# Moving eighteen conditioning broadcasts, four LayerNorm affines and one last affine in a two-layer encoder kernel

## The reference

```python
c_act = jax.nn.silu(c)
for layer in range(DEPTH):
    mod = c_act @ cond_w[layer] + cond_b[layer]
    sh_m, sc_m, g_m, sh_f, sc_f, g_f = [m[:, None, :] for m in jnp.split(mod, 6, axis=-1)]
    h = x * (1.0 + sc_m) + sh_m
    y = mixer(h)
    x = layer_norm(ALPHA * x + g_m * y, ln_w[layer, 0], ln_b[layer, 0])
    h = x * (1.0 + sc_f) + sh_f
    y = feed_forward(h)
    x = layer_norm(ALPHA * x + g_f * y, ln_w[layer, 1], ln_b[layer, 1])
```

## Time and profile before

| | us |
|---|---|
| Runs | 1716.56, 1714.35, 1717.05; median 1716.56 |
| The profiled execution | 1716.56 |
| Its span | 1714.7 |
| PE busy in the span | 1615.6 (94%) |
| DVE busy | 1286.5 (75%) |
| ACT busy | 1008.3 (59%) |
| POOL busy | 134.3 (8%) |

### The profile page before, as it was taken

How to read it: one execution, slowest core, us unless ns; L and a number is a source line. 1 busy time by engine, 2 the same in 40 slices (tenths; PEclk the granted TensorE clock), 3 DMA queues, 4 the chain that set the end, 5 groups by cost and what they waited for, 6 DMA issues and landing times.

```text
span 1714.7 us, 20084 instructions
## 1 busy us (share of the span) xinstructions
PE 1615.6 (94%) x7810; PEld 1292.7 (75%) x7810; DVE 1286.5 (75%) x1162; ACT 1008.3 (59%) x867; POOL 134.3 (8%) x92
## 2 busy tenths in 40 slices
PE   4888999999999999789999999999999999999996
PEld 1774766788868777578888888888888888888875
DVE  1384638655467665788898898898898888998987
ACT  0432225444444544357777777777777777777775
POOL 0330402020001001210000000000000000000004
PEclk8997999999999999889999999999999999999998
DMA  9347996965445444479999999999999999999994
GB/s 328 138 150 269 320 356 206 297 218 197 169 157 175 154 148 171 147 258 389 384 382 386 375 389 382 374 388 373 381 390 370 385 389 370 389 385 361 388 377 157
DMA packets 234370, 515.33 MB, mean 301 GB/s; under 512 B 8936, under 2 KB 40960, under 8 KB 234176
## 3 DMA queue, kind: packets, MB, share of 16 engines
q1 hardware_dynamic: 228272, 491.99, 78.6%
q0 software_dynamic: 3008, 10.20, 1.9%
q10 hardware_dynamic: 2992, 11.79, 1.9%
HBM read 507.15 MB, written 13.11 MB: 303 GB/s over the span
## 4 chain that ended last, share of the span: by engine, by line
PE 87%; DVE 7%; issue 2%; ACT 2%; DMA 2%; POOL 0%; POOLq 0%; SPq 0%; DVEq 0%
PE bank L759 26%; PE bank L761 25%; PE bank L760 25%; PE bank L738 2%; PE bank L924 2%; DMA ring<-in_cond_w 2%; PE bank L1188 1%; PE bank L754 1%; DVE arena L1791 1%; DVE w_part L1650 0%; ACT w_part L1315 0%; PE bank L1170 0%; PE bank L855 0%; DVE w_lo L1661 0%; PE bank L1179 0%
## 5 line engine op out<-in xcount | busy, mean ns | idle before, releaser
L1661 DVE TENSOR_TENSOR w_lo<-ring,w_hi 128x2048 fp32r<-128x2048 f32 x336 | 765.0, 2290 | 104.4 <-ACT w_hi L1544 102.9
L1544 ACT ACTIVATE w_hi<-ring 128x2048 fp32r<-128x2048 f32 x334 | 640.5, 1918 | 196.8 <-PE bank L761 187.1
L759 PE MATMUL bank<-w_lo,heT_hi 128*128 128x512 f32 x896 | 353.9, 395 | 3.8 <-DVE w_lo L1661 2.2
L761 PE MATMUL bank<-w_hi,heT_hi 128*128 128x512 f32 x896 | 349.7, 390 | 0.0
L760 PE MATMUL bank<-w_hi,heT_lo 128*128 128x512 f32 x896 | 348.9, 389 | 0.0
L1650 DVE TENSOR_TENSOR w_part<-ring,w_part 128x1024 fp32r<-128x1024 f32 x148 | 185.5, 1262 | 180.1 <-ACT w_part L1315 173.1
L1315 ACT ACTIVATE w_part<-ring 128x1024 fp32r<-128x1024 f32 (+1 forms) x162 | 168.9, 1049 | 233.5 <-PE bank L761 228.2
L759 PEld LDWEIGHTS bank<-w_lo,heT_hi 128*128 128x128 f32 x896 | 168.3, 188 | 39.0 <-issue 5.9
L761 PEld LDWEIGHTS bank<-w_hi,heT_hi 128*128 128x128 f32 x896 | 168.2, 188 | 35.9
L759 PE MATMUL bank<-w_part,hT_hi 128*128 128x512 f32 (+1 forms) x448 | 178.2, 398 | 17.8 <-DVE w_part L1650 12.3
L760 PEld LDWEIGHTS bank<-w_hi,heT_lo 128*128 128x128 f32 x896 | 168.4, 188 | 33.5
(11 more groups left out here) (342 smaller groups left out, 1586.7 us busy)
## 6 DMA issues: line engine op xcount, KB each, us to landing
ring<-in_moe_w_up SPq DMA_DIRECT2D x224, 1024.0 KB, 8.5
ring<-in_moe_w_down SPq DMA_DIRECT2D x112, 1024.0 KB, 7.9
ring<-in_cond_w SPq DMA_DIRECT2D x24, 2048.0 KB, 9.1
ring<-in_ffn_w_up SPq DMA_DIRECT2D x22, 1024.0 KB, 7.9
ring<-in_od_w_in SPq DMA_DIRECT2D x8, 2048.0 KB, 8.0
ring<-in_ev_w_in SPq DMA_DIRECT2D x5, 2048.0 KB, 12.4
ring<-in_ffn_w_down SPq DMA_DIRECT2D x5, 2048.0 KB, 7.9
ring<-in_od_w_in SPq DMA_DIRECT2D x8, 1024.0 KB, 8.0
```

The source lines that it names most:

```text
L759: mm(bank, lhs[0], rhs[1], start=start, stop=False)
L761: return mm(bank, lhs[0], rhs[0], start=False, stop=stop)
L1544: f(w_hi[:, n % 3], half_landed(act, it, u, half), ACT.Copy) \
L1661: tt(w_lo[:, buf], at, w_hi[:, buf].bitcast(F32), ALU.subtract).then_inc(S["w_lo"], 1)
```

## The change

- `MIX_COND` and `END_COND` go. Their 18 pieces are spread elsewhere: (0, 6) and (0, 7) after level 3, (0, 8) and (0, 9) after level 4; ten pieces in feed-forward up, one after each unit from unit 1 to unit 10; two in feed-forward down, ahead of units 2 and 4; (1, 10) and (1, 11) after `od_qk` of heads 1 and 2. The ScalarE evictions stand at the matching places of its stream.
- The affines of stages 0 and 1 move from their places in the loops into `stage_end`: after the transposed copies DVE makes one more low part, the affine of tile 0, one more low part, the affine of tile 1, and waits for it. ScalarE's wait before the gates goes.
- In stage 3 the affine of tile 0 moves from DVE to POOL, with a semaphore `first_done`, on which SyncE waits before it sends out tile 0. DVE does tile 1.

The hunks of `pe_order()` are left out below; they list the same moves.

```diff
@@ -127,9 +127,10 @@
 BATCH_OF = {key: b for b, batch in enumerate(COND_BATCHES) for key in batch}
 
 ROWS_LEVEL = 1
-LEVEL_COND = {2: (4, 5)}
-MIX_COND = (6, 7, 8, 9)
-END_COND = (((0, 10), (0, 11), (1, 0), (1, 1), (1, 2), (1, 3)), tuple((1, u) for u in range(4, 10)), ((1, 10), (1, 11)))
+LEVEL_COND = {2: (4, 5), 3: (6, 7), 4: (8, 9)}
+UP_COND = {0: (0, 10), 1: (0, 11), 2: (1, 0), 3: (1, 1), 4: (1, 2), 5: (1, 3), 6: (1, 4), 7: (1, 5), 8: (1, 6), 9: (1, 7)}
+DOWN_COND = {0: (1, 8), 2: (1, 9)}
+OD_COND = {0: 10, 1: 11}
 
 
 def stream_units():
...
@@ -711,7 +714,7 @@
             over_loop(sp, over_count(sp), over_item)
             for t in range(NT):
 
-                sp.wait_ge(S["ln_done"], 3 * NT + t + 1)
+                sp.wait_ge(S["ln_done" if t else "first_done"], 3 * NT + 1 if t else 1)
                 sp.dma_start(out[0, t * P:(t + 1) * P, :], xs[:, t]).then_inc(S["out_done"], 16)
             sp.wait_ge(S["out_done"], 16 * NT)
 
@@ -1029,12 +1032,8 @@
                 last.then_inc(full, 1)
             cond_rows(len(cond_order) - rows_next[0])
             turn(1, lambda half, t: taken(pe, "pv", t) if half else pe.wait_ge(S["mix_ready"], t + 1), (2, 3, 0, 1))
-            for u in MIX_COND:
-                cond(0, u)
             project(("ev_out", 0), 1)
             project(("ev_out", 1), 1, steps=LAST)
-            for key in END_COND[0]:
-                cond(*key)
             turn(2, h_ready(1), BY_TILE[:2])
 
             def down(kind, lhs, n_units, n_chunks, between):
@@ -1075,6 +1074,8 @@
             for u in range(FFN // 256):
                 project(("ffn_up", u), 2, steps=None if u else FIRST,
                         second=None if u else lambda: turn(2, h_ready(1), BY_TILE[2:]))
+                if u - 1 in UP_COND:
+                    cond(*UP_COND[u - 1])
                 if u:
                     ffn_turn(u - 1)
 
@@ -1082,11 +1083,11 @@
 
                 if i == 1:
                     ffn_turn(FFN // 256 - 1)
+                if i > 1 and i - 2 in DOWN_COND:
+                    cond(*DOWN_COND[i - 2])
                 taken(pe, "ffn_T", min(2 * i + 1, FFN // 256 - 1))
 
             down("ffn_down", (ffT_hi, ffT_lo), 6, FFN // P, ffn_between)
-            for key in END_COND[1]:
-                cond(*key)
             turn(3, h_ready(2), BY_TILE[:2])
             def weighted_values(g):
 
@@ -1112,6 +1113,8 @@
             for h in range(RH):
                 project(("od_qk", h), 3, steps=None if h else FIRST,
                         second=None if h else lambda: turn(3, h_ready(2), BY_TILE[2:]))
+                if h - 1 in OD_COND:
+                    cond(1, OD_COND[h - 1])
                 if h:
                     weighted_values(h - 1)
                 project(("od_v", h), 3)
@@ -1144,8 +1147,6 @@
                     taken(pe, "ret_yT", i, t)
 
             down("od_out", (yT_hi, yT_lo), 4, RH * RV // P, od_between)
-            for key in END_COND[2]:
-                cond(*key)
             turn(4, h_ready(3), BY_TILE)
 
             pe.wait_ge(S["nw_lo"], 2)
@@ -1280,9 +1281,7 @@
 
                 if l == 1:
 
-                    if u < 4:
-                        act.wait_ge(S["h_ready"], 4)
-                    elif u < 10:
+                    if u < 10:
                         act.wait_ge(S["h_ready"], 8)
                     else:
                         act.wait_ge(S["ln_done"], 4)
@@ -1425,22 +1424,15 @@
                 for t in range(NT):
                     act.wait_ge(S["resid_var"], NT * stage + t + 1)
                     f(rstd[:, t:t + 1], aggr[:, t, 1:2], ACT.Sqrt, bias=eps_ln).then_inc(S["resid_rstd"], 1)
-                    keys = END_COND[stage] if stage < 3 and t == 0 else ()
-                    for key in keys[:1]:
-                        cond(*key)
                     act.wait_ge(S["norm_in"], NT * stage + t + 1)
                     f(xs[:, t], hs[:, t], ACT.Identity, bias=shift_n[:, t:t + 1], scale=rstd[:, t:t + 1]) \
                         .then_inc(S["normed"], 1)
-                    for key in keys[1:]:
-                        cond(*key)
                     if turn_rows:
                         turned(stage + 2, BY_TILE[2 * t:2 * t + 2])
 
             turned(1, (2, 3, 0, 1))
             cond_kept(2)
             split_to(part_no["ev_out", 0, 0] + BUFS)
-            for u in MIX_COND:
-                cond(0, u)
             for u in range(2):
                 split_ahead("ev_out", u)
             normalise(0, True)
@@ -1486,7 +1484,6 @@
                 for t in range(NT):
                     copy(("ret_T", h, t), r_qT[:, :, t * P:(t + 1) * P], heads)
                 split_ahead("od_g", h)
-                act.wait_ge(S["ln_done"], 2 * NT)
                 for t in range(NT):
                     if h >= 2:
 
@@ -1747,14 +1744,11 @@
                     to_normalise(stage, 1)
                     modulated(1)
                     turned(stage + 2, BY_TILE)
-                if not part_left:
-                    affines(stage)
-
-            def affines(stage, tiles=range(NT)):
-
-                for t in tiles:
+                for t in range(NT):
+                    if part_left:
+                        split_to(part_left + 3 + t)
                     affine(stage, t)
-                dve.wait_ge(S["ln_done"], NT * stage + tiles[-1] + 1)
+                dve.wait_ge(S["ln_done"], NT * stage + NT)
 
             def narrow_lo(w, n):
                 dve.wait_ge(S["nw_hi"], n)
@@ -1995,8 +1989,6 @@
                     tt(ff_a[:, u % 2, t], ff_s[:, u % 2, t], bank[:, 256:512], ALU.mult).then_inc(free, 1)
                 if u:
                     ffn_turned(u - 1)
-                if 1 <= u <= NT:
-                    affines(0, (u - 1,))
             for i in range(6):
                 if i < 5:
                     split_ahead("ffn_down", i)
@@ -2056,11 +2048,7 @@
                 if h:
                     head_norm(h - 1)
                 split_ahead("od_v", h)
-                if h == 0:
-                    affines(1, (0,))
                 split_ahead("od_g", h)
-                if h == 0:
-                    affines(1, (1,))
                 bank, free = filled(dve, "ret_s", h)
                 V.do(tt(r_s[:, 0:2 * P], bank[:, 0:2 * P], ret_d[:, h], ALU.mult))
                 tt(r_s[:, 2 * P:3 * P], bank[:, 2 * P:3 * P], ret_d[:, h, 0:P], ALU.mult).then_inc(free, 1)
@@ -2230,7 +2218,6 @@
             V.do(add_back(count + LAST_ITEM, 1, 1, hs))
             moments(1)
             to_normalise(3, 1)
-            affine(3, 0)
             affine(3, 1)
 
 
@@ -2374,6 +2361,10 @@
                 pool.wait_ge(S["weighed"], t + 1)
                 G.then(tt(xs[:, t], xs[:, t], picked[0][:, t], ALU.add))
                 tt(xs[:, t], xs[:, t], picked[1][:, t], ALU.add).then_inc(S["base_ready"], 1)
+            pool.wait_ge(S["ln_in"], 32 * 4)
+            pool.wait_ge(S["normed"], 3 * NT + 1)
+            G.then(tt(xs[:, 0], xs[:, 0], ln[:, 0], ALU.mult))
+            tt(xs[:, 0], xs[:, 0], ln[:, 1], ALU.add).then_inc(S["first_done"], 1)
 
 
 
```

More of the change, by code:

```diff
@@ L183, in pe_order @@
     o += [("go", t) for t in range(NT)] + [("cond_rows", 2)]
-    o += [("hT", 1, i) for i in (2, 3, 0, 1)] + [("cond", 0, u) for u in MIX_COND]
+    o += [("hT", 1, i) for i in (2, 3, 0, 1)]
     o += [("ev_out", u, t) for u in range(2) for t in range(NT)]
-    o += [("cond", *key) for key in END_COND[0]] + [("hT", 2, i) for i in BY_TILE[:2]]
+    o += [("hT", 2, i) for i in BY_TILE[:2]]
     for u in range(FFN // 256):
-        o += [("ffn_up", u, t) for t in range(NT)] + ([] if u else [("hT", 2, i) for i in BY_TILE[2:]])
+        o += [("ffn_up", u, t) for t in range(NT)] + ([] if u else [("hT", 2, i) for i in BY_TILE[2:]]) + ([("cond", *UP_COND[u - 1])] if u - 1 in UP_COND else [])
         o += [("ffn_T", u - 1)] if u else []
     o += [("ffn_down", t, h) for t in range(NT) for h in range(2)] + [("ffn_T", FFN // 256 - 1)]
-    o += [("cond", *key) for key in END_COND[1]] + [("hT", 3, i) for i in BY_TILE[:2]]
+    o += [("cond", *key) for key in DOWN_COND.values()]
+    o += [("hT", 3, i) for i in BY_TILE[:2]]
     for h in range(RH):
@@ L194, in pe_order @@
         if h:
+            o += [("cond", 1, OD_COND[h - 1])] if h - 1 in OD_COND else []
             o += [("ret_y", h - 1, t) for t in range(NT)]
@@ L201, in pe_order @@
     o += [("ret_y", RH - 1, t) for t in range(NT)] + [("ret_yT", RH - 1, t) for t in range(NT)]
-    o += [("cond", *key) for key in END_COND[2]] + [("hT", 4, i) for i in BY_TILE]
+    o += [("hT", 4, i) for i in BY_TILE]
     o += [("routerT",), ("router",), ("rank",)]
@@ L265 @@
     "turn_hi rows_hi nw_hi nw_lo piece_used act_hi tok_hi picked_in0 picked_in1 out_done "
-    "weighed_by scaled weighed base_ready hot_made hot_turned hot_taken result_gated back_full back_free "
+    "weighed_by scaled weighed base_ready hot_made hot_turned hot_taken result_gated back_full back_free first_done "
```

## The result

The changed kernel took 1739.2 us (median of 4 runs, 1739.0 to 1739.76) against 1716.8 for the kernel before (4 runs, 1714.35 to 1719.65): 1.0131 times as long, 95% interval 1.0113 to 1.0148, so 19.4 to 25.4 us slower. The prediction was 1740.4, in a range from 1730 to 1747. The profiled execution has a span of 1738.2 us, 23.5 more than before; that is the amount that the traces can take apart.

A forecast was written before the change was run, and what follows sets the result against it. TensorE, busy 94% of the span and without gaps in the long stretches, was taken as the bound. 3.8 - 0.2 + 10.8 + 0 + 0 + 1.9 + 1.6 + 5.5 + 0.4 = 23.8 us gave 1740.4, range 1730 to 1747.

The forecast's parts named there:

- Levels: Level stage: four broadcasts added behind levels 3 and 4, where TensorE has no slack, cost +3.8 us.
- feed-forward: Feed-forward up and down: ten and two broadcasts added where TensorE is always busy, 9.0 and 1.8, together +10.8 us.
- Mixer projection: Start of the mixer projection: four broadcasts leave, but DVE's first low part is ready only near 267.7; gain 0.2 us.
- Clock: End of stage 0 and mixer projection: idle left by moved broadcasts drops TensorE to half rate, +1.9 and +1.6 us.
- Clock, the terms set to 0: Ends of stages 1 and 2: already idle long enough before the change, so no added low-clock cost, 0.
- Affines: Stages 0 and 1: moved affines delay DVE's next low parts, TensorE waits 2.0 and 3.5 us, total +5.5.
- The end: Kernel's end: POOL's affine of tile 0 disturbs DVE's work on tile 1; +0.4 us, between -1.05 and +1.6.
- (a): Stages 0 and 1: weight parts are further ahead than counted, so the affines are hidden; 1734.9 us, chance 0.12.
- (b): Stage 0 end and mixer projection: TensorE's clock stays full despite the idle; 1736.9 us, chance 0.12.
- (d): All of TensorE: busy records hide weight waits, so moved broadcasts and affines cost nothing; about 1717 us, chance 0.05.
- (e): Stage ends: broadcasts and evictions set their length, so moving them makes the kernel faster; 1712.6 us, chance 0.04.
- (c): Retention broadcasts visible, mixer projection's low clock twice as long, DVE lateness passed on; 1745.8 us or more, chance 0.07.

The follow-up runs named there:

- fillers: Changed kernel plus dummy broadcasts, results unread, where moved ones stood (four before mixer projection; six, six, two at stage ends): 1736.7 us, ratio 1.0125; again 1736.24, ratio 1.0123.
- the late load: Kernel before with only affines of stages 0 and 1 moved, POOL's stage 1 LayerNorm weight load held until feed-forward up unit 2 is evicted: 1720.8 us, ratio 1.0037.
- the heads: Kernel before with DVE's od_v and od_g parts placed around and inside the head norm, broadcasts (0, 4), (0, 5) moved into the state scan: 1707.69 us, ratio 0.9960.

## Why the prediction was right

The forecast of 1740.4 stands 1.2 us above the median, and the mechanism of nearly every step holds in the traces. That the sum, 23.8, is within 0.3 of the 23.5 measured is luck in part. Levels, feed-forward, clock and affines were set 2.2 too high in all; the projection, the end and a low clock that was not foreseen, 2.9 too low; and the start and the experts, which no edit touches, took 1.0 less.

- **Levels** (3.8): 3.4, twice, in the changed kernel and alone. A broadcast costs 0.85 from start to start; the 1.91 of the earlier trace rows for two includes an end that the next instruction overlaps. The same makes the 10.8 of **feed-forward** 10.3, or 10.5 with the stage ends alone.
- **Mixer projection** (-0.2): 0. It begins when DVE's part is ready; nothing is gained.
- **Retention broadcasts** and **stage ends** (0): 0, by the run with two broadcasts alone and by 7.88 against 7.87 at the end of stage 1.
- **Clock** (1.9 and 1.6): 1.5 and 1.5, both with 0.50 where it was forecast, and both undone by fillers, which gave 3.1 back by the trace. The price of 1.9, taken from stage 1, belongs to a low stretch that ends 6.8 us behind the first transpose; in stage 0 it ended 6.1 behind it. The Trainium skill ("TensorE: Matmul & The Clock Gate", Part 1) says that an idle stretch returns the clock to half rate; the traces agree at 270.62 and 299.44.
- **Clock, the terms set to 0**: this was wrong by 2.2. "Stages 1 and 2 are idle long enough already: 0" misses that the price depends on where the low stretch ends. Behind the first transpose of stage 1 it lasts 8.4 us instead of 6.8, and the stage takes 11.71 instead of 11.01. The longer wait is not shown to be the cause: the runs with levels alone, with the late load and with the heads have the old wait of 2.34 there, a low stretch of the old length that ends 8.3 to 8.5 behind the first transpose, and 11.67 to 11.78. And the fall in head 3, 1.5, was not foreseen at all.
- **Affines** (5.5): the place and the number of waits are as forecast, two, two and one more behind the rotation. They cost 1.9 and 2.8 against 2.0 and 3.5. In stage 1 the waits are 0.67, 0.48 and 0.97 as recorded, where 1.0, 1.0 and 1.5 were counted. (The prediction's 4.34 us for 18 matmuls would be 2.9 a part; from start to start a part is 2.72, near the 2.7 that it used.) Alone the affines cost more, 7.2, by a path that the prediction did not follow: what the affine's semaphore releases on POOL.
- **The end** (0.4): +0.9 and +0.85. The mechanism is the one named: a small instruction of tile 1 held behind POOL's first operation, and DVE's affine longer (one of its two instructions, not both). The split between the bounds -1.05 and +1.6 was set 0.5 too low.
- **The rivals**: (a) is refuted by the waits of the affine runs, (b) by the granted clock and by what the fillers gave back, (d) and (e) by the ratios of the runs with levels or ends alone. Of (c) only its kind of cause, more low clock than counted, was seen, in stage 1 and head 3 instead of the mixer projection.

Run alone, the parts cost more than together. By the traces, without the start and the experts, the affines take 6.4, the levels 7.3, the stage ends 12.9 and the last affine 0.9, 27.5 in all, where the changed kernel has 24.5. Of the 3.0 between, 1.8 is the wait for the late weights, which the changed kernel hasn't, and 0.7 a low clock that ends later in stage 0 with the stage ends alone; the 0.4 left lies mostly in stage 1.

**What stays open** is the fall in head 3. In all five profiles of the changed kernel, filled or not, the clock fell at 660 to 664, behind the wait of 2.09. It fell at 648.2 with the level broadcasts alone, also behind the wait of head 3, and at 561.9 with the late load, behind that of head 1. But the kernel before has the same wait, three times, and shows 1.00 throughout, as do the affines alone, the last affine alone, the ends alone and the two broadcasts alone. Counted over these profiles, 7 of 22 waits of 2.09 or 2.10 in the heads were followed by half rate, and none of 14 of 1.23 or 1.24. What tells the 22 apart was not found; fillers elsewhere don't change it. So of the 23.5 us, 2.2 are low clock that no edit was shown to cause. A kernel with head 3's wait removed from the changed kernel was not tried.

## What to carry to other kernels

Where an engine is busy without a gap, work moved into its queue costs its own length, and what it leaves behind at a wait for another engine returns nothing: compare the end of the wait, not its length. A filler in such a wait may still be worth its place where it keeps the clock up, as in two of the three places here where the price was expected. An affine, or any work that is needed later, belongs where the engine's products are some buffers ahead, and before it is moved earlier, everything that its semaphore releases is to be followed, transfers above all.

## What the hardware showed unexpectedly

- Equal waits of TensorE, 2.09 to 2.10 us, were followed by the full clock in the kernel before and by 3.4 us at 0.50 in the changed one. At the end of stage 1 the same wait of 2.34 cost 0.7 more where the low stretch ended 1.5 us later.
- Beside a POOL operation on SBUF, a DVE instruction on one column took 1.02 instead of 0.16, and ended within 0.02 of the POOL operation, in the run with the last affine alone as well. The rows look as if the two took turns, whole operations at a time: the DVE part at 277.46 of the earlier trace rows took 2.10 beside a POOL operation that ended at 278.48, and the next POOL operation, at 278.56, took 2.15, where that before it took 1.29. A DVE reciprocal beside the same POOL operation (one input, at 1729.11) kept its 0.16. That they take turns is read from these rows and was not tested.
- A wait of 0.72 between matmuls moved what follows by 1.0: 315.55 to 319.28 is 3.73, where a part takes 2.72. In a run of matmuls the starts are 0.23 apart and each record is 0.39 long, so a recorded gap begins 0.16 later than the delay does.
- A load of LayerNorm weights (one row each of weight and bias, spread by DMA), issued some 25 us earlier, made two units of the weight stream land some 3 us later in all six profiles that have it; with the affines alone that took TensorE 1.8 us.
